# A two-layer block on one core: half of the 64x64 turns as transposes, and a new order of the work around the mixer's solve and its second attention pair

## The reference

```
p = rms_norm(x) @ w_in                       # 15 column blocks of 256 (one is small)
o_a = softmax attention with decays (fox)    # 4 heads, tokens in 2 tiles of 128
o_b = gated delta rule, chunks of 64 (gdn)   # m = strict lower part; solve (I + m) w = ..., then a scan over 4 chunks
o_c, o_d = gated linear attention (hg, gla)  # 4 + 4 heads, by pairs of tokens with decays
x = x + concat(norm(o_a), norm(o_b) * silu(z), norm(o_c) * silu(g), norm(o_d) * silu(g)) @ w_out
x = x + (silu(gate) * up) @ w_down           # and two more layers
```

## Time and profile before

| | |
|---|---|
| median of 3 runs | 1060.12 us (1058.24 to 1060.25) |
| the profiled execution | 1060.12 us, of which its span is 1058.3 us |
| busy TensorE | 1034.3 us, 98% of the span |
| busy VectorE | 842.9 us, 80% |
| busy ScalarE | 627.1 us, 59% |
| granted TensorE clock | 0.995 of full speed (2.4 GHz) |

### The profile page before, as it was taken

One profiled execution on the slowest core, in us unless ns is written; L12 is line 12 of the kernel. 1 busy time (PEld: TensorE's weight loads), 2 busy tenths in 40 slices (PEclk: granted clock), 3 DMA queues, 4 the chain that ended last, 5 costly groups with the idle time before them and its releaser, 6 DMA issues.

```text
span 1058.3 us, 20780 instructions
## 1 busy us (share of the span) xinstructions
PE 1034.3 (98%) x8321; PEld 962.7 (91%) x8321; DVE 842.9 (80%) x1192; ACT 627.1 (59%) x858; POOL 5.8 (1%) x16
## 2 busy tenths in 40 slices
PE   7999999999999999999999999999999999999996
PEld 6999989999999998899999999989999998999985
DVE  6966687589988876877998888779675799988875
ACT  6664464476656555545665555677576576555565
POOL 0000000000000000000000000000000000000000
PEclk9999999999999999999999999999999999999999
DMA  9432222454655545464556555444434355655531
GB/s 331 157 121 82 81 82 82 173 192 166 205 191 198 179 160 176 162 237 141 191 199 204 192 198 168 151 160 159 154 126 143 116 199 186 211 190 177 188 120 40
DMA packets 26290, 174.35 MB, mean 165 GB/s; under 512 B 3133, under 2 KB 3413, under 8 KB 6000
## 3 DMA queue, kind: packets, MB, share of 16 engines
q1 hardware_dynamic: 25520, 171.17, 47.0%
q0 software_dynamic: 704, 2.23, 0.7%
HBM read 172.33 MB, written 1.06 MB: 164 GB/s over the span
## 4 chain that ended last, share of the span: by engine, by line
PE 77%; DVE 4%; ACT 3%; issue 1%; DVEq 0%; ACTq 0%
PE PS L526 67%; PE PS L477 10%; DVE w_lo L2131 2%; ACT w_hi L1409 1%; DVE h_both L2144 0%; DVE x L2674 0%; PE PS L1319 0%; DVE arena L2670 0%; ACT h_both L1426 0%; ACT xn L1481 0%; DVE arena L2517 0%; ACT arena L1953 0%; DVE arena L2668 0%; DVE arena L2866 0%; PE PS L734 0%
## 5 line engine op out<-in xcount | busy, mean ns | idle before, releaser
L526 PE MATMUL PS<-h_both,w_hi 128*128 128x512 f32 (+1 forms) x1808 | 486.1, 344 | 10.0 <-DVE w_lo L2175 7.3
L2131 DVE TENSOR_TENSOR w_lo<-raw,w_hi 128x2048 fp32r<-128x2048 f32 x156 | 357.1, 2290 | 65.4 <-ACT w_hi L1409 60.3
L526 PE MATMUL PS<-h_both,w_lo 128*128 128x256 f32 (+1 forms) x1384 | 373.4, 282 | 0.0
L526 PEld LDWEIGHTS PS<-h_both,w_hi 128*128 128x128 f32 x1808 | 307.2, 189 | 55.4 <-DVE w_lo L2175 7.3
L1409 ACT ACTIVATE w_hi<-raw 128x2048 fp32r<-128x2048 f32 x157 | 299.5, 1909 | 88.6 <-PE PS L526 73.2
L526 PEld LDWEIGHTS PS<-h_both,w_lo 128*128 128x128 f32 (+1 forms) x1384 | 257.4, 190 | 0.3
L526 PE MATMUL PS<-act_hi,w_lo 128*128 128x256 f32 x704 | 197.8, 282 | 0.0
L526 PE MATMUL PS<-act_hi,w_hi 128*128 128x256 f32 x704 | 197.8, 282 | 0.0
L526 PE MATMUL PS<-act_lo,w_hi 128*128 128x256 f32 x704 | 194.9, 282 | 0.0
L526 PEld LDWEIGHTS PS<-act_hi,w_hi 128*128 128x128 f32 x704 | 133.2, 189 | 2.2 <-issue 1.1
L526 PEld LDWEIGHTS PS<-act_hi,w_lo 128*128 128x128 f32 x704 | 132.3, 188 | 0.2 <-issue 0.2
(11 more groups left out here) (337 smaller groups left out, 1119.9 us busy)
## 6 DMA issues: line engine op xcount, KB each, us to landing
raw<-weights SPq DMA_DIRECT2D x157, 1024.0 KB, 4.9
arena<-masks_in SPq DMA_DIRECT2D x1, 1472.0 KB, 11.7
x<-x_in SPq DMA_DIRECT2D x4, 256.0 KB, 4.2
raw<-weights SPq DMA_DIRECT2D x4, 256.0 KB, 5.4
raw<-weights SPq DMA_DIRECT2D x2, 512.0 KB, 8.7
arena<-bias_by_distance POOLq DMA_DIRECT2D x1, 1024.0 KB, 8.3
result<-arena SPq DMA_DIRECT2D x4, 256.0 KB, 2.0
arena<-p_in POOLq DMA_DIRECT2D x2, 256.0 KB, 4.7
```

Source lines behind the costliest of these rows:

```text
L526: return pe.matmul(o, lhs, rhs, start=start, stop=stop, skip_group_check=True)
L2131: tt(w_lo[:, slot, :], raw[:, slot, :], w_hi[:, slot, :].bitcast(F), ALU.subtract).then_inc(lo_ready, 1)
```

## The change

It has five parts. In `turn_chunks` the product of the rows 0 to 63 becomes a transpose. TensorE: the turn of the hg keys goes ahead of the second pair's logits, and a quarter of block 12 that stood behind `fox_values(1)` is done together with the last quarter inside `la_all`. ScalarE: the copy of the turned keys and the second pair's exponentials go ahead of `block_hi(13)`. VectorE in the levels: `fox_sums` and half of block 9's low part stand ahead of level 0, the other half behind level 0's update; block 10's two halves and `fox_scale` go behind their levels' updates where they stood ahead. VectorE behind the levels: `block_lo(13)` and `la_clear` go behind `fox_out(1)`; the two clears change places, and the wait between them is gone.

```
--- before.py
+++ after.py
@@ -885,7 +885,10 @@
                 for u in range(8):
                     for c in range(2):
                         r = rows_of_chunk(c)
-                        last = mm(chunk_bank(bank, u, c), v[r, u, :], ident[r, r])
+                        if c == 0:
+                            pe.transpose(chunk_bank(bank, u, c), v[r, u, :], ident[r, r])
+                        else:
+                            last = mm(chunk_bank(bank, u, c), v[r, u, :], ident[r, r])
                 return last
 
             def gdn_turn_decay():
@@ -1087,7 +1090,7 @@
                 pe.wait_ge(sem("la_keys"), 1)
                 la_pairs(-1)
                 la_exponents(0, 1)
-                quarter(BLOCK_OF["gdn_z"], 3)
+                project(BLOCK_OF["gdn_z"], 1)
                 for lv in range(8):
                     if lv < 6:
                         la_exponents(lv // 2 + 1, lv % 2)
@@ -1165,14 +1168,13 @@
             gdn_state_out(2)
             quarter(11, 3)
             gdn_state_in(3)
+            la_turn_keys()
             fox_logits(1)
             gdn_state_out(3)
-            la_turn_keys()
             quarter(12, 0)
             fox_turn_probs(1)
             quarter(12, 1)
             fox_values(1)
-            quarter(12, 2)
             la_all()
             la_out()
 
@@ -1761,9 +1763,9 @@
             la_parts()
             la_keys()
             fox_copy(0)
+            la_turn_keys()
+            fox_exps(1)
             block_hi(13)
-            fox_exps(1)
-            la_turn_keys()
             fox_copy(1)
             tokens_from(BLOCK_OF["gla_v"])
             la_exps(0, 0)
@@ -2478,9 +2480,8 @@
                    ALU.subtract).then_inc(sem("la_split"), 1)
 
             def la_clear():
+                mark(dve.memset(a_la[CHUNK:P, :, 0:CHUNK], 0.0))
                 mark(dve.memset(a_packed, 0.0))
-                dve.wait_ge(sem("fox_probs_turned"), 2)
-                mark(dve.memset(a_la[CHUNK:P, :, 0:CHUNK], 0.0))
                 signal(sem("pairs_free"), 1)
 
             def la_all():
@@ -2580,20 +2581,23 @@
             gdn_grams()
             gdn_first_inverse()
             gdn_first_turned()
-            block_lo(9)
+            fox_sums()
+            half_lo(9, 0)
             for lv in range(5):
                 if lv < 4:
                     gdn_next_block(lv)
                 else:
                     gla_queries_and_keys()
                     block_lo(11)
-                if lv in (1, 2):
-                    half_lo(10, lv - 1)
+                gdn_xcx(lv)
+                if lv == 0:
+                    half_lo(9, 1)
+                if lv == 1:
+                    half_lo(10, 0)
+                if lv == 2:
+                    half_lo(10, 1)
                 if lv == 3:
                     fox_scale()
-                gdn_xcx(lv)
-                if lv == 0:
-                    fox_sums()
             dve.memset(state, 0.0).then_inc(sem("state_ready"), 1)
             gdn_state_in(0)
             fox_max(0)
@@ -2606,14 +2610,14 @@
             fox_out(0)
             gdn_state_out(2)
             la_parts()
-            block_lo(13)
             gdn_state_in(3)
             scale_queries()
             fox_max(1)
             gdn_out()
-            la_clear()
             fox_out(1)
             dve.sem_inc(sem("group_out"), 1)
+            la_clear()
+            block_lo(13)
             la_all()
             gate_gains(2, 1)
             mixed_lo((0, 1))
```

## The result

The changed kernel took 1072.88 us (median, 1070.85 to 1073.01), the kernel before 1059.18 us in the same comparison: ratio 1.0125, 95% interval 1.0107 to 1.0143, 13.7 us between the medians, 1.25% slower by the ratio. Forecast were 1064.0 us and at most 1066.8. The direction was right, the size was not.

What follows compares the result with a forecast made beforehand. TensorE, busy for 98% of the span, was taken to bound the kernel. From 1060.12 us, transposes -0.3, VectorE's levels +2.2 and second attention pair +2.0 gave +3.9 us: 1064.0 us, range 1060.9 to 1066.8.

Steps and rivals of the forecast that it cites:

- the transposes: In TensorE's two turns, replacing 8 of 16 products each was to save 0.3 us for both.
- the count of 32 ns a record: In each turn, 24 records in place of 32 at 32 ns: 0.25 us less, 0.5 us for both.
- the upper end: In the turns, transposes overlapping no product come on top of the products: +0.4 us a turn, +0.8 us for both.
- drains: Rival, chance 0.08: in the turns, each transpose/product change costs 0.11 us, 3.5 us in place of 0.3 saved; 1067.8 us.
- the three waits in the levels: TensorE waits for VectorE ahead of block 9, block 10 and the solve: 0.7, 0.7, 0.7 to 0.8; +2.2 us.
- the second pair: Around the second attention pair, later exponentials, copy, `fox_out` and clears delay the first level's pairs by +2.0 us.
- The term for the clears: Both VectorE clears, now behind `fox_out(1)`, make the first pairs start at 130.75 instead of 129.46: +1.3 us.
- A shift at 135 us arrives at the end unchanged: Behind the mixer nothing is touched and earlier work releases everything, so delay at 135 us reaches the end in full.

Runs made afterwards that it cites:

- before_filled: Kernel before plus products of zeros in TensorE's four waits in the attention levels: 1058.24 us against 1058.33, ratio 0.9995.
- pair_pe_only: Kernel before with only TensorE's two edits around the second attention pair, ScalarE's and VectorE's lists as before: 1059.28 us against 1058.57, ratio 1.0006.
- turns_only: Kernel before with only the transposes, alternating with products in both turns: 1063.23 us against 1058.52, ratio 1.0043.
- turns_grouped: Kernel before with the transposes, all eight ahead of the eight products in each turn: 1059.87 us against 1058.52, ratio 1.0015.
- turns_products_grouped: Kernel before without transposes, each turn's eight products of one row half ahead of the other half's eight: 1059.91 us against 1058.57, ratio 1.0019.

## Why the prediction was wrong

- **Failed: the transposes.** The term was -0.3 us, "nearer to the record count, since the same list of matmuls gets shorter", with ends of -0.5 and +0.8. It measured +4.8 us, far outside. Two steps of it failed. First, the count of 32 ns a record: the time of a turn was not its number of records but the products of one row half, 1.07 us, beside which the other half ran free; taking records from the free half could save nothing. The text named that overlap only for the upper end. Second, the upper end had each transpose wait for its neighbours but left out the change of kind, though the rival "drains" had it, at 3.5 us and 1067.8 us, with a chance of 0.08. The rival had the right mechanism as far as the runs go, a price at each change of kind: 0.13 us as measured, 0.11 us as read from the earlier trace rows, where it counted 16 changes a turn and there are 15. What a change is in the array stays open. That full transposes and f32r matmuls join without a loss was no evidence for 64x64 tiles, and it should not have held the chance so low.
- **Right: the three waits in the levels.** Forecast 0.7, 0.7 and 0.7 to 0.8 us, +2.2 in all; measured 0.67, 0.67 and 0.7, +2.05.
- **Right: the second pair.** Forecast +0.4 at the turn, +0.95 at the values, +0.4 at the exponents, +1.3 at the first pairs and +2.0 at the first level. Counted from the last state product (117.39 before, 125.00 after) they were +0.4, +0.75, +0.35, +1.8 and, less the half clock, +2.4. The term for the clears was too small by 0.5 us: VectorE's timeline shows the first clear only 0.48 us behind `fox_out` and the second 0.28 us behind the first, where the earlier trace rows gave 0.16 and I took none between them.
- **Missing: the clock.** The prediction says nothing of the granted clock. At full clock the changed kernel is 9.0 us slower (one execution on the second chip); the median measured was 13.7 us slower (1072.88 - 1059.18). The rest goes with more half clock: in the profiled execution it was one stretch, 1.5 us; the timed executions had mean clocks of 0.991 to 0.994. Where their stretches lay was not recorded; the traces show such ones behind the turns and behind the waits of the second pair. The kernel before showed its own stretch at 154 us in the very trace that I read, as pairs and a projection that took nearly twice their time, and I read past it.
- "A shift at 135 us arrives at the end unchanged" held for the work; it did not for the clock, which a shift can move into or out of a stretch.

With -0.3 put right to +4.8, the sum is 1060.12 + 4.8 + 2.2 + 2.0 = 1069.1 us, close to the profiled 1069.26 us, but partly by chance: it has the half clock of before in its base and leaves out the one of after.

**A version that beats both?** None by the median. before_filled has the median of the kernel before (1058.24 and 1058.33 us), and what it takes away are the executions from 1059.4 to 1060.8 us. No part of the change that was run alone was faster, and of the lists pair_pe_only costs least, 0.7 us, with an interval that includes none.

## What to carry to other kernels

Count what runs side by side before counting instructions: if products of two row halves overlap in the array, making one half cheaper saves nothing, and mixing transposes with products costs at every change. On a list that is just in time, a helper's work moved behind an update is paid for by the engine that waits, but for the few tenths of slack (0.67 us for a half block of 1.23 us moved), so ask of each moved piece who needs it and how many tenths there are. And look at the granted clock in the trace of before, and of more than one execution: the new order of the second pair cost 2.4 us by its work and waits, and in two traces 1.5 or 2.0 us of half clock on top.

## What the runs showed of the hardware

- A change between a 64x64 transpose of 32-bit floats and a 64x64 product costs 0.13 us where the two lie in different row halves, with the tile's size in the rows unchanged (turns_only against turns_grouped); eight such transposes in a row take 0.07 us each.
- Eight 32-bit products of 64x64 in one row half take 1.07 us (turns_grouped); sixteen, alternating between the halves, 1.02 to 1.08 us (the kernel before); sixteen, half by half, 1.83 us (turns_products_grouped).
- Stretches of 3.4 to 7 us at half clock (1.2 of 2.4 GHz) came behind waits of 0.2 to 1.3 us, and also behind stretches in which TensorE is recorded as busy all the time: the alternating turns, in two of five traces, and sixteen products of four columns, in one. The same instructions ran at full clock in other executions. In the attention levels ten products of zeros, 2.2 us of work laid into waits, kept it away in eleven of eleven executions (before_filled).
